# Neighbourhood attention in a two-block transformer kernel: the softmax division moves from VectorE to GpSimd, and the reciprocal to the head of the next step

## The reference, cut to what matters

```
s = jnp.einsum('bcqhd,bicjhd->bhcqij', q_row, k_win).astype(F32) * scale
s = s + jnp.transpose(bias, (0, 2, 3, 1, 4))[None]
s = jnp.where(valid[None, None, :, :, None, :], s, NEG)
p = jax.nn.softmax(s.reshape(s.shape[:4] + (kh * band,)), axis=-1)
p = p.reshape(s.shape).astype(v.dtype)
return jnp.einsum('bhcqij,bicjhd->bcqhd', p, v_win)
```

## Time and profile before

| | us |
|---|---|
| median of 3 runs | 1287.24 (1286.85 to 1287.76) |
| the profiled execution's own time | 1286.42 |
| its span in the trace | 1284.5 |
| TensorE busy | 1263.0 (98%) |
| VectorE busy | 786.6 (61%) |
| ScalarE busy | 647.9 (50%) |
| GpSimd busy | 216.9 (17%) |

### The profile page before, as it was taken

One profiled execution on the slowest core, in us unless ns is written; L12 is line 12 of the kernel. 1 busy time (PEld: TensorE's weight loads), 2 busy tenths in 40 slices (PEclk: granted clock), 3 DMA queues, 4 the chain that ended last, 5 costly groups with the idle time before them and its releaser, 6 DMA issues.

```text
span 1284.5 us, 16448 instructions
## 1 busy us (share of the span) xinstructions
PE 1263.0 (98%) x6004; PEld 1045.6 (81%) x6004; DVE 786.6 (61%) x1465; ACT 647.9 (50%) x1261; POOL 216.9 (17%) x234
## 2 busy tenths in 40 slices
PE   9999999999999999999999999999999999999998
PEld 8887888878888888888787777887888888888887
DVE  6689687686645565356788876589644343343334
ACT  6787788554335433233555655586533252332344
POOL 0064555000100011001002101032311030110111
PEclk9998999999999999999999999999999999999999
DMA  7211110423333323332333212432333324233332
GB/s 275 86 50 34 42 41 26 170 82 99 90 100 98 98 90 99 99 96 68 115 91 98 76 56 68 131 112 68 98 99 92 97 75 118 79 115 89 100 90 67
DMA packets 64626, 118.20 MB, mean 92 GB/s; under 512 B 7713, under 2 KB 12193, under 8 KB 64289
## 3 DMA queue, kind: packets, MB, share of 16 engines
q1 hardware_dynamic: 62704, 112.86, 29.3%
q10 hardware_dynamic: 1840, 4.29, 1.1%
HBM read 115.02 MB, written 2.10 MB: 91 GB/s over the span
## 4 chain that ended last, share of the span: by engine, by line
PE 90%; DVE 4%; ACT 2%; issue 2%; DMA 1%; POOL 1%; POOLq 0%; SPq 0%; DVEq 0%; ACTq 0%
PE bank L593 26%; PE bank L595 25%; PE bank L594 25%; PE bank L813 2%; PE bank L693 2%; PE bank L694 2%; PE bank L695 2%; PE bank L826 1%; PE bank L827 1%; PE bank L799 1%; PE bank L800 1%; PE bank L767 1%; DVE q2p L2191 0%; DMA praw<-in_pT 0%; DVE r_bc L2086 0%
## 5 line engine op out<-in xcount | busy, mean ns | idle before, releaser
L2022 DVE TENSOR_TENSOR wl<-raw,wh 128x512 fp32r<-128x512 f32 (+2 forms) x360 | 267.5, 754 | 325.5 <-ACT wh L1323 324.8
L1323 ACT ACTIVATE wh<-raw 128x512 fp32r<-128x512 f32 (+1 forms) x398 | 242.2, 618 | 284.7 <-PE bank L595 273.7
L593 PE MATMUL bank<-AH,wh 128*128 128x512 f32 (+1 forms) x848 | 333.8, 394 | 2.1 <-DVE AL L2036 0.8
L595 PE MATMUL bank<-AH,wl 128*128 128x512 f32 (+1 forms) x848 | 329.3, 388 | 0.0
L594 PE MATMUL bank<-AL,wh 128*128 128x512 f32 (+1 forms) x848 | 327.0, 386 | 0.0
L593 PE MATMUL bank<-BH,wh 128*128 128x512 f32 x624 | 247.7, 397 | 1.6 <-ACT acc L1533 1.6
L595 PE MATMUL bank<-BH,wl 128*128 128x512 f32 x624 | 244.6, 392 | 0.0
L594 PE MATMUL bank<-BL,wh 128*128 128x512 f32 x624 | 243.0, 389 | 0.0
L595 PEld LDWEIGHTS bank<-AH,wl 128*128 128x128 f32 x848 | 159.6, 188 | 35.8
L593 PEld LDWEIGHTS bank<-AH,wh 128*128 128x128 f32 x848 | 159.9, 189 | 35.2 <-issue 2.9
L594 PEld LDWEIGHTS bank<-AL,wh 128*128 128x128 f32 x848 | 159.7, 188 | 33.0 <-issue 0.2
(11 more groups left out here) (332 smaller groups left out, 1617.4 us busy)
## 6 DMA issues: line engine op xcount, KB each, us to landing
raw<-in_w_dn SPq DMA_DIRECT2D x104, 256.0 KB, 2.7
raw<-in_w_gu SPq DMA_DIRECT2D x88, 256.0 KB, 2.6
raw<-in_w_up SPq DMA_DIRECT2D x64, 256.0 KB, 2.6
raw<-in_w_nsa SPq DMA_DIRECT2D x16, 256.0 KB, 2.7
raw<-in_w_pg SPq DMA_DIRECT2D x16, 256.0 KB, 2.7
raw<-in_w_naq SPq DMA_DIRECT2D x16, 256.0 KB, 2.7
nbi<-in_na_bias ACTq DMA_DIRECT2D x8, 448.0 KB, 3.4
raw<-in_w_swa SPq DMA_DIRECT2D x10, 256.0 KB, 2.7
```

Source lines behind the costliest of these rows:

```text
L593: t.matmul(o, w, xh, start=start, stop=False, skip_group_check=skip)
L595: return t.matmul(o, wl, xh, start=False, stop=stop, skip_group_check=skip)
L1323: a.activation(W[i % NW].h[:, 0:n], RAW[i % NRAW][:, 0:n], ACT.Copy).then_inc(*s_wh.up(i))
L2022: v.tensor_tensor(w.l[:, 0:n], RAW[i % NRAW][:, 0:n], w.h[:, 0:n], ALU.subtract).then_inc(*s_wl.up(i))
```

## The change

On VectorE, `norm` is gone. The reciprocal of unit s-1 is issued first in step s, before `soft` of unit s, with the wait for the exponentials of unit s-1 ahead of it. On GpSimd, four multiplications (by the reciprocal and by a column of ones) are issued per step ahead of the low parts of the weights of that step. TensorE's transposes wait for GpSimd's semaphore instead of VectorE's. The function of the first block is only rewritten.

```diff
                 if 1 <= s <= 8:
-                    turn(NA, ("na", s - 1), PP2[(s - 1) % 2], s_nm)
+                    turn(NA, ("na", s - 1), PP2[(s - 1) % 2], s_nmg)
...
-            def norm(L, u, pp, s4):
-                e.wait_ge(s_ex.at(u))
-                v.reciprocal(s4, s4).then_inc(*s_nm.up(("r", u)))
-                e.wait_ge(s_nm.at(("r", u)))
-                for qb in range(4):
-                    o = pp[:, L["off"][qb]:L["off"][qb] + L["w"][qb]]
-                    v.tensor_scalar(o, o, s4[:, qb:qb + 1], None, ALU.mult).then_inc(*s_nm.up((u, qb)))
...
             for s in range(10):
+                if 1 <= s <= 8:
+                    s4 = S4[(s - 1) % 6]
+                    e.wait_ge(s_ex.at(("na", s - 1)))
+                    v.reciprocal(s4, s4).then_inc(*s_nm.up(("r", ("na", s - 1))))
                 if s < 8:
...
-                if 1 <= s <= 8:
-                    norm(NA, ("na", s - 1), PP2[(s - 1) % 2], S4[(s - 1) % 6])
...
+            def norm(L, u, pp, s4, by):
+                e.wait_ge(s_nm.at(("r", u)))
+                for qb in range(4):
+                    o = pp[:, L["off"][qb]:L["off"][qb] + L["w"][qb]]
+                    g.tensor_scalar(o, o, s4[:, qb:qb + 1], by(qb), ALU.mult, ALU.mult).then_inc(*s_nmg.up((u, qb)))
...
-            for s in range(10):
-                for name, i in FILL2.get(s, ()):
+            for s in range(1, 11):
+                if s <= 8:
+                    norm(NA, ("na", s - 1), PP2[(s - 1) % 2], S4[(s - 1) % 6], one)
+                for name, i in FILL2.get(s - 1, ()):
                     lo(WHERE[name, i] + 4)
```

More of the change, by code:

```diff
@@ L2958, in gpsimd, with one @@
             g.memset(chid[1][:, :], 0.0).then_inc(*s_z.up("zero"))
+            def norm(L, u, pp, s4, by):
[3 more added lines that the diff above has]
+                    g.tensor_scalar(o, o, s4[:, qb:qb + 1], by(qb), ALU.mult, ALU.mult).then_inc(*s_nmg.up((u, qb)))
+            def one(qb):
+                return ones[:, 0:1]
             def norm1(u):
[L2961 to L2964, removed]
+                if unit(u)[0] == "swa":
+                    norm(SWA, u, probs(u), S4[u % 6], one)
+                else:
                     e.wait_ge(s_dv.at("gv"))
[L2966 to L2969, removed]
+                    norm(NSA, u, probs(u), S4[u % 6], lambda qb: gate_of(u)[:, qb:qb + 1])
             for s in range(1, N_UNITS + 3):
```

## The result

The changed kernel takes 1291.24 us (median of 6 runs, 1289.97 to 1293.38), the kernel before beside it 1287.05 us (6 runs, 1285.31 to 1289.05). The ratio is 1.0033 with a 95% interval of 1.0020 to 1.0046: slower by 2.6 to 5.9 us. The forecast was 1287.6, within 1285.9 to 1289.3. The time lies outside, on the side of the rival that the prediction called "Slower" and gave a chance of 0.08.

A forecast was written before the change was run, and what follows sets the result against it. TensorE bounds the kernel (98% busy), the VectorE and ScalarE loop from 863 on. Later stalls less saved transpose waits give about +0.45: 1286.42 becomes 1286.9, plus 0.8 for the median 1287.7, rounded to 1287.6; range 1285.9 to 1289.3.

The forecast's parts named there:

- Slower: Rival: head wait and both meetings in steps 1 to 3 make `soft` of unit 5 over 3 us late; +2 to +4, chance 0.08.
- The wait at the head of step 1: VectorE: unit 0's reciprocal waits for ScalarE ahead of `soft` of unit 1, which starts 2.65 us later.
- That lag: Late `soft` of units 5 to 7 (about 1.0, 1.2, 1.5 us) delays TensorE; about +0.45 at the fill, carried to the end.
- the cost of the earlier meeting: VectorE's subtractions, now earlier, overlap GpSimd's weight pieces: 0.5 us for a step's first meeting, 1.3 for a second.
- I take the first alone: Only the first meeting counted in step 1, 0.5 us: `soft` of unit 2 at 840.2, 2.2 us late.
- The argument against the second one: GpSimd's second weight piece misses VectorE's subtraction by 0.1 us in each step; TensorE's pace until 867 gives `soft` room.
- The step that followed from it: VectorE's loop, steps 2 to 4: `soft` lag falls to 1.25 us at unit 3, 0.8 at unit 4, about 1.0 at unit 5.
- until 867 its steps have slack and nothing changes: TensorE's steps before the stall at 868.40 absorb the late `soft`, so no time is lost there.
- The stall at 868.40: TensorE's scores of unit 6, held 1.05 us by VectorE's bank readout L2214; to end 0.9 to 1.0 us later.
- The wait for L2207 near 883: TensorE waits before unit 6 for `rest` of unit 5, behind `soft` of unit 7; to grow to about 1.5 us.
- With no second lag: Branch of the sum: `soft` of unit 2 from 839.7, giving 0.9 us less: -0.5.
- the branch with both meetings: Both meetings in step 1: `soft` of unit 2 at 841.6, lag 2.4 at unit 5, sum +1.8 us.

The follow-up runs named there:

- e3: Changed kernel with ScalarE copying queries or keys ahead of both weight copies in steps 1 to 4; stage -1.40 us, ratio 0.9990 against the kernel before.
- e8: Kernel before with four repeated subtractions added on VectorE in step 4, ahead of the bank read; stage +3.25 us, ratio 1.0022 against the kernel before.
- e4: Kernel before without reciprocals and divisions, transposes waiting for the exponentials, probabilities not normalised; stage -1.74 us, ratio 0.9987 against the kernel before.
- e1: Changed kernel with the reciprocal back behind `rest` of unit s-2, multiplications still on GpSimd; stage +3.52 us, ratio 1.0027 against the kernel before.
- e5: Changed kernel with the reciprocal of unit 0 behind `soft` of unit 1 again, others at the head; stage +0.50 us, ratio 0.9997 against the kernel before.
- e2: Kernel before with only the reciprocal moved to the head of the step, division still on VectorE; stage +2.90 us, ratio 1.0027 against the kernel before.

## Why the prediction was wrong

**Right.** The wait at the head of step 1 was priced at 2.65 us and measured 2.56; the exponentials of unit 1 were to end at 836.8 and end there (838.57 less 1.75). GpSimd's four multiplications take 2.38 us (2.4 predicted), not 3.30, and no transposes wait for them. The transposes of units 6 and 7 win the 0.56 and 0.37 us; those of unit 4 win 0.34 of 0.65, since they begin at the lower clock (0.50 in 878 to 879; 1.25 us in e3, at 1.00). That lag turns into time one to one behind step 5 holds (e8). That it is L2206 or L2214, the head output, on which TensorE stalls, holds too.

**The step that failed** is the cost of the earlier meeting, in the words "I take the first alone": 0.5 us was taken for step 1, and the meetings there cost 1.80. `soft` of unit 2 was put at 840.2 with one meeting, at 841.6 with both; it is at 841.23. The argument against the second one was that GpSimd's second piece misses by 0.1 us in each step. The profile after has it at 841.00, and the query subtraction before it ends at about 841.02 (0.55 behind 840.47): a first meeting stretches VectorE's first subtraction just so far that the next weight piece is there. In all four steps of this profile a second one follows the first. e4 shows the other branch, in step 3 (rows above): its first subtraction ends at about 856.12 (0.55 behind 855.57), GpSimd's second piece comes at 856.18, a little too late to get in, and it is GpSimd that is held (1.82 us instead of 1.30); VectorE's pair takes 2.01 us. So a few hundredths of a microsecond decide, and a margin of 0.1 us between two engines' starts was no ground for leaving the second meeting out.

**The step that followed from it** put nothing in for meetings in steps 2 to 4: the lag was to fall to 1.25 by unit 3, 0.8 by unit 4 and 1.0 by unit 5, as VectorE has 1.27 us less in each step. It was 3.27, 3.94 and 4.02: VectorE's relief of 1.27 us per step was eaten by meetings of 1.65 to 1.80. And "until 867 its steps have slack and nothing changes" was wrong by 1.33 us, since a lag of over 3 us is more than that slack. The stall at 868.40 was to grow by 1.0 and grew by 2.65, which with the 1.33 ahead of it makes the 3.98. The wait for L2207 near 883, forecast at 1.5 us, is not there at all: TensorE was later than VectorE's `rest` by then.

**Sums that don't come out.** Step 2 is 10.29 - 1.27 + 0.2 = 9.22, not 9.35. 839.7 with both meetings (0.5 + 1.3) is 841.5, not 841.6. "With no second lag" takes 0.9 off for a `soft` that is 0.5 us earlier, while the branch with both meetings adds its 1.4 one to one; by the same rule it would be 0.5. For unit 7, 0.9 less 0.37 is 0.5 to 0.6, and the 0.45 leans on "rounding". None of them would have brought the forecast near 1291.24.

**The rival "Slower"** named the mechanism, the place, the sign of the decision and a price of 2 to 4 us (3.56 in the stage, 4.19 between the medians; a stall of 3.70 where it said over 4). Its low chance rested on the same 0.1 us and on TensorE's pace; the meeting at 865.51, which the text itself cites, was direct evidence for it and should have weighed more.

**What stays open.** Why executions enter the stage up to 2 us apart. And 3.56 us is one execution against one; the runs say 2.6 to 5.9. Of e1's 3.52 us the waits for GpSimd are shown, but not how much each is worth.

## What to carry to other kernels

When work leaves an engine, look not at its busy time but at which operations of other engines it now runs beside; here 10 us less on VectorE cost 3.6 us, and the same change with one wait on GpSimd wins 2.5. If two engines block each other in some kind of operation, price a meeting at up to the length of the other's operation (0.67 to 1.04 us for pieces of 1.30 here), and price a second one behind the first as well; then order the copies that release them so that one engine's come first. A sum whose branches lie 0.1 us apart in start times has no likeliest branch.

## What was not expected of the hardware

- A subtraction of VectorE with both operands in SBUF does not share with one of GpSimd, it ends 0.55 us behind the end of GpSimd's, wherever in it it began: 1.36, 1.73, 1.37 and 1.66 us instead of 0.69. GpSimd gets in between two subtractions of VectorE's queue that stand back to back (3.20 us for a pair). It goes the other way too: with VectorE's L2211 (881.00, 0.69 us) inside them, GpSimd's four multiplications in e1 take 2.93 us instead of 2.38 (879.83).

  The Trainium skill (SBUF — State Buffer, section Who interferes with whom) describes the ports that both share as a lock that one engine holds at a time, and says that a VectorE instruction with two SBUF inputs contends with a GpSimd instruction that reads SBUF. The trace agrees, by the numbers above.
- `soft`, which reads one operand from PSUM, is not slowed by GpSimd's multiplications beside it: in the profile after 0.42 us for 256 columns at 834.86 and 0.55 for 384 at 835.21, inside GpSimd's 834.67 to 837.05; before, with GpSimd idle, 0.42 and 0.55 as well.
- TensorE's granted clock stayed at 1.00 through the stall of 1.05 us before, and was lower in or behind stalls of 1.83 us (e5, 0.62 in 870 to 874), 2.99 (e2, 0.64 in 874 to 877), 3.70 (after, 0.50 from 873 to 879) and 3.95 (e8, 0.50). Low for over six microseconds, it cost 0.3 to 0.4 us (0.35 by e8, 34.47 against 34.15 for after and e3): TensorE needs about 1 us more up to the transposes of unit 4 (4.67 against 3.70) and gets most of it back where it would have waited. e3 waits 1.06 us for L2200 in front of the values of unit 6, after doesn't.
